# Mixing stage: the short convolution's chunks ahead of the attention's, the long convolution by channel halves, score groups every second slot from the 17th

## The chip, the cores and the metric

The kernel runs on one core of one Trainium2 chip. The metric is the device time of one execution in microseconds (us); lower is better.

## What is computed

A residual stream of 256 tokens by 1024 features goes through two layers of a first block and two layers of a second block. The change is in the first block's mixing stage, run once in each of its two layers. All data are float32.

```python
u = rms_norm(h, mix_pre_g[l])
(a_b, a_c, a_x, b_u, c_q, c_k, c_v, d_q, d_k, d_v, d_f, gate_logits) = _split(u @ w_in[l], IN_SPLITS)
y_a = (a_b * causal_depthwise_conv(a_c * a_x, a_conv_w)) @ a_w_out             # 3 taps, 512 channels
y_b = conformer_conv_mixer(b_u, ...)   # a * sigmoid(g), 31 taps on 512 channels, layer norm, silu, @ b_w_out
y_c = diff_attention_mixer(...)        # 4 heads, two softmaxes each, their difference @ v, rms norm, @ c_w_out
y_d = forgetting_attention_mixer(...)  # 8 heads, bias from a cumulative sum of log_sigmoid(d_f), @ d_w_out
g = sigmoid(gate_logits).reshape(bsz, seq, 4, D_MODEL)
merged = g[:, :, 0] * y_a + g[:, :, 1] * y_b + g[:, :, 2] * y_c + g[:, :, 3] * y_d
h = h + rms_norm(merged @ w_o[l], mix_post_g[l])
```

## The kernel before

**Chunks.** All weights stream through SBUF in 270 chunks of up to 128 x 2048 numbers, in the order `LOAD`, into a ring of `SLOTS = 5` buffers. SP issues the load of a chunk as soon as TensorE has used the chunk five earlier (L515). Each product is made of three fp32r products: ScalarE copies a chunk into `whi` (`split`, L575), VectorE subtracts it from the raw chunk into `wlo` in the raw chunk's place (`split`, L905), and `mm3` (L1433 to L1435) issues the three matmuls for each tile. The splits run `AHEAD = 3` chunks before their use.

**The mixing stage** has 47 slots, one chunk each: 23 `cols` chunks (`w_in` without the gates, in the order of the tuple `COLS`, whose numbers name the chunk: 14, 15, 0 and 1 to 3 are u and the long convolution's inputs with 0, 1 its gate halves; 4, 5, 6, 7 the short convolution's `a_c` and `a_x`; 8, 9 its `a_b`; 10 to 15 q, k, v of the first attention; 16 to 21 those of the second; 22 the forget logits; chunks 14 and 15 are taken by a routine of their own before slot 2), then 24 merge chunks: for each branch in the order a, c, d, b and each half of the features two `gate` chunks and one `out` chunk.

**Order of the work.** `mix_steps()` writes the steps between the chunks by hand: `at(slot, step)` puts a step ahead of that slot's chunk, and `rank` orders the steps of one slot. Every engine walks through the one list `MIX` and issues its own part of each step, in order; semaphores carry the rest. So within a slot

- TensorE does its transposes and small matmuls of the steps, then the slot's chunk (48 matmuls);
- ScalarE does its part of the steps, then empties the chunk's bank (an evacuation; L694 to L718, or a tanh, L728), then splits the chunk three slots on (L575);
- VectorE does its part of the steps, then what it has of the chunk (a masked product for `cols` 2, 3, 6, 7; the gated sum of an `out`, L1075 to L1080), then its split of the chunk three slots on (L905), which needs ScalarE's.

**The attention** goes in eight groups. Groups 0 to 3 are the first attention (0, 1 the first 128 queries with one tile of keys; 2, 3 the second 128 with two), 4 to 7 the second attention (4, 5 with two tiles of keys; 6, 7 with one). A group has four steps, in this kernel one slot after the other:

- `scores`: TensorE's score matmuls (L1675), VectorE's bias, maximum and its negation (L1178 or L1185, L1188, L1190), ScalarE's four exponentials (L768);
- `weigh`: VectorE's reciprocals and, in groups 0 to 3, the difference of the two softmaxes (L1198, L1201, L1205; L1210 in the others);
- `turn`: TensorE transposes the weights (L1690), ScalarE copies them (L775). TensorE waits for `p_ready` of this group's `weigh` and for `o_read` of the group before, which its `values` gives;
- `values`: TensorE's products with v (L1704), VectorE's normalization (L1218, L1223).

```python
                        pe.wait_ge(p_ready, l * 8 + (g + 1))
                        if g:
                            pe.wait_ge(o_read, l * 8 + g)
```

The first attention's output is then normalized (`o_norm` on ScalarE, L781, and POOL; `o_scale` on VectorE, L1232 and L1234), and all outputs are transposed (`flip`, L1716) and split (`o_split`, L789 and L1242). `conv` is one tap of the long convolution, four instructions on VectorE (L1094, L1096) and a drain behind them, `a_conv` one of the short one (L1108, L1110, L1114). Before slot 22's successor, the first gate chunk, TensorE waits for the evacuation of slot 22, since both use bank 0:

```python
                        if j:
                            pe.wait_ge(th_ready, l * 16 + ((j - 1) * 2 + part + 1))
                        else:
                            cols_taken(pe, l, COLS[22 - part])
```

Of the kernel before, what the change touches and what calls it, by code (L numbers as in the profile page):

```python
# [30 lines left out]
KH = HID // P  # L31
# [6 lines left out]
A_CONV = 3  # L38
B_CONV = 31
# [51 lines left out]

COLS = (14, 15, 0, 1, 2, 3, 22, 10, 11, 12, 13, 4, 5, 6, 7, 8, 9, 16, 17, 18, 19, 20, 21)
BRANCH = (0, 2, 3, 1)
HCOLS = (0, 1, 2, 5, 6, 7, 3, 4, 8, 9, 10, 11, 12, 13)

# [21 lines left out]
def mix_steps():  # L119
    before = {}  # L120

    def at(slot, *step):
        before.setdefault(slot, []).append(step)

    for tap in range(B_CONV):
        at(6 + tap * 28 // B_CONV, "conv", tap)
    for tap in range(A_CONV):
        at(15 + tap, "a_conv", tap)
    at(18, "a_split")
    at(35, "ln_stats")  # L130
    at(36, "ln_apply")
    at(38, "ln_back")
    at(39, "ln_silu")
    at(40, "ln_split")
    at(8, "f_turn")
    at(9, "f_log")
    at(10, "f_tok")
    at(12, "f_sum")
    at(13, "f_store")
    at(19, "f_load")  # L140
    at(21, "f_mask", 1)
    for g, s in enumerate((12, 14, 16, 18, 22, 24, 27, 29)):
        at(s, "scores", g)
        at(s + 1, "weigh", g)
        at(s + 2, "turn", g)
        at(s + 3, "values", g)
    at(25, "f_mask", 0)
    for i, s in enumerate((18, 22)):
        at(s, "o_norm", i)
        at(s + 1, "o_scale", i)  # L150
    for i, s in enumerate((21, 25, 29, 34)):
        at(s, "flip", i)
        at(s, "o_split", i)
    chunks = [("cols", i) for i in COLS]
    for b in range(4):
        for half in range(2):
            chunks += [("gate", b, half, 0), ("gate", b, half, 1), ("out", b, half)]
    rank = {"ln_stats": 0, "ln_apply": 0, "ln_back": 0, "ln_silu": 0, "weigh": 0, "values": 1, "flip": 2, "o_split": 3,
            "f_turn": 4, "f_sum": 4, "f_mask": 4, "turn": 5, "scores": 6}
    steps = []  # L160
    for slot, chunk in enumerate(chunks):
        steps += sorted(before.pop(slot, []), key=lambda x: rank.get(x[0], 8))
        steps.append(chunk)
    assert not before, before
    return steps


MIX = mix_steps()


# [70 lines left out]
def program(nc, stream, x_in, pre_gain, post_gain, par1, par2, cst_in, out):  # L241
    ctx = ExitStack()
    with ctx:
# [8 lines left out]
        at = nc.sbuf_base  # L252
# [29 lines left out]
        def area(a, n):  # L282
            return mix[:, a:a + n]
# [8 lines left out]
        PB = T + B_CONV - 1  # L292
        PA = T + A_CONV - 1
        pad_b = area(3072, KH * PB).rearrange("p (m t) -> p m t", m=KH)
        otok = [area(a, 1024).rearrange("p (a n) -> p a n", a=2) for a in (1024, 9336)]
        decay = area(5240, 2048).rearrange("p (e k) -> p e k", e=8)
        acc_b = area(4216, 1024).rearrange("p (m t) -> p m t", m=KH)
        lnt = area(4216, 1024).rearrange("p (t n) -> p t n", t=NT)
# [94 lines left out]
        conv_done = sem("conv_done")  # L393
# [501 lines left out]
        def _(dve):  # L895
# [121 lines left out]
            for l in range(DEPTH):  # L1017
# [22 lines left out]
                for step in MIX:  # L1040
                    kind = step[0]
                    if kind == "cols":
                        i = step[1]
                        p = COLS.index(i)
# [18 lines left out]
                    elif kind == "gate":  # L1063
                        _, b, half, part = step
                        at = AT_MERGE + (b * 2 + half) * 3 + part + AHEAD
                        split(ch + at)
                    elif kind == "out":
                        _, b, half = step
# [17 lines left out]
                                op0=ALU.mult, op1=ALU.subtract).then_inc(m_ready, 1)  # L1086
                        split(c + AHEAD)
                    elif kind == "conv":
                        tap = step[1]
                        for m in range(KH):  # L1090
                            w = pr1("b_conv")[:, m * B_CONV + tap:m * B_CONV + tap + 1]
                            v = pad_b[:, m, tap:tap + T]
                            if tap == 0:
                                ins = TS(acc_b[:, m, :], v, w, pr1("b_bias")[:, m:m + 1], ALU.mult, ALU.add)  # L1094
                            else:
                                ins = STT(out=acc_b[:, m, :], in0=v, scalar=w, in1=acc_b[:, m, :], op0=ALU.mult,  # L1096
                                          op1=ALU.add)
# [4 lines left out]
                    elif kind == "a_conv":  # L1102
                        tap = step[1]
# [63 lines left out]
                    elif kind == "scores":  # L1167
                        g = step[1]
# [22 lines left out]
                    elif kind == "weigh":  # L1191
                        g = step[1]
                        w, t, _ = group1(g)
# [18 lines left out]
                    elif kind == "values":  # L1212
                        g = step[1]
# [24 lines left out]
                    elif kind == "o_split":  # L1238
                        i = step[1]
# [9 lines left out]
            for l in range(DEPTH):  # L1249
# [40 lines left out]
                for step in HYB:  # L1290
# [3 lines left out]
                    elif kind == "chunk":  # L1294
                        _, p, i, half = step
# [7 lines left out]
                    elif kind == "a_norm":  # L1303
# [5 lines left out]
                        for t in range(NT):  # L1309
                            hyb_taken(dve, l, 2)  # L1310
                            x = z[:, t, Z_AQ:Z_AV].rearrange("p (e d) -> p e d", e=8)
                            for e0, e1, o in ((0, 6, 0), (6, 8, 128)):
                                a, b = (v[:, 64 * e0:64 * e1].rearrange("p (e d) -> p e d", d=64) for v in (thb, tmp))
# [44 lines left out]
                    elif kind == "scores":  # L1358
                        g = step[1]
# [21 lines left out]
                    elif kind == "weigh":  # L1381
                        g = step[1]
# [13 lines left out]
                    elif kind == "values":  # L1396
                        g = step[1]
# [28 lines left out]
        def _(pe):  # L1426
# [152 lines left out]
            for l in range(DEPTH):  # L1579
# [4 lines left out]
                for step in MIX:  # L1584
                    kind = step[0]
                    if kind == "cols":
                        i = step[1]
                        p = COLS.index(i)
# [5 lines left out]
                        if i == 22:  # L1594
                            s = c % SLOTS
# [9 lines left out]
                    elif kind == "gate":  # L1605
                        _, b, half, part = step
# [8 lines left out]
                    elif kind == "out":  # L1615
                        _, b, half = step
# [12 lines left out]
                        s = c % SLOTS  # L1629
# [5 lines left out]
                                          k == KH - 1)  # L1635
                        ins.then_inc(used, 1)
                    elif kind == "ln_stats":
                        pe.wait_ge(conv_done, l + 1)
                        for t in range(NT):
                            for m in range(KH):  # L1640
                                ins = pe.transpose(bank(4 + t)[:, m * P:(m + 1) * P], acc_b[:, m, t * P:(t + 1) * P],
# [22 lines left out]
                    elif kind == "scores":  # L1664
                        g = step[1]
# [6 lines left out]
                        for e in range(4):  # L1672

                            m, p0 = hp * 2 + e // 2, 64 * (e % 2)
# [3 lines left out]
                    elif kind == "turn":  # L1678
                        g = step[1]
                        w, t, _ = group1(g)  # L1680
# [6 lines left out]
                        n = 0  # L1687
# [322 lines left out]
```

## Time and profile before

| | |
|---|---|
| time, median of 3 runs | 1797.87 us (1796.89 to 1797.89) |
| the profiled execution's own time | 1796.47 us |
| its span | 1794.7 us |
| TensorE busy | 1707.2 us, 95% |
| VectorE busy | 1088.7 us, 61% |
| ScalarE busy | 800.2 us, 45% |
| mixing stage, end of slot 1 to end of slot 46 | 303.5 us in the first layer, 305.0 us in the second |

The profile is one execution. Its times are from the first to the last instruction; the execution's own time is 1.8 us longer. PE is TensorE's matmuls, PEld its weight loads, DVE VectorE, ACT ScalarE, POOL GpSimd. PEclk is the share of full speed that TensorE's clock was granted. A row that ends in [4.80 <-DVE mix L1218] says that the engine sat idle for 4.80 us before it, and that the instruction named released it.

### The profile page before, as it was taken

The numbers are of one execution on the slowest core, as the hardware profiler recorded it, in microseconds if no ns is written. First come the engines' busy times: TensorE is split into PE (matmuls) and PEld (weight loads), VectorE is DVE, ScalarE is ACT, GpSimd is POOL, SyncE is SP. The second block draws the span as 40 slices with busy tenths as digits, with TensorE's granted clock in tenths as the row PEclk, the third lists the DMA queues.
The fourth block names the chain that finished last, engine by engine and source line by source line (L and its number), as shares of the span: only waits on it lengthen the run. The fifth ranks groups of instructions, "written<-read, shape, count | busy, mean of one in ns | idle before, by whom it ended". The sixth has DMA issues, their size and how long they took to land.

```text
span 1794.7 us, 28417 instructions
## 1 busy us (share of the span) xinstructions
PE 1707.2 (95%) x12340; PEld 1597.0 (89%) x12340; DVE 1088.7 (61%) x1271; ACT 800.2 (45%) x1053; POOL 34.0 (2%) x60
## 2 busy tenths in 40 slices
PE   6999999789999999999999988999999999889987
PEld 6999899789999999899989978999999988679866
DVE  5454667777666444654466777766744466556554
ACT  5333544444444433534344444444533445544552
POOL 0000000000000000000000000000000000000000
PEclk9999999999999999999999989999999999999989
DMA  7555554334445555555545433445555542215120
GB/s 277 186 187 186 184 214 144 139 130 152 180 173 212 187 186 181 204 188 182 186 174 211 165 124 134 144 181 180 201 188 188 183 170 101 95 42 196 63 94 24
DMA packets 43358, 293.14 MB, mean 163 GB/s; under 512 B 4817, under 2 KB 5217, under 8 KB 10465
## 3 DMA queue, kind: packets, MB, share of 16 engines
q1 hardware_dynamic: 39744, 278.94, 43.1%
q10 hardware_dynamic: 3488, 12.38, 2.0%
q8 instruction: 98, 1.61, 0.4%
q14 instruction: 28, 0.22, 0.0%
HBM read 290.23 MB, written 1.06 MB: 162 GB/s over the span
## 4 chain that ended last, share of the span: by engine, by line
PE 81%; DVE 8%; ACT 7%; DVEq 2%; issue 2%; DMA 1%; POOL 0%; ACTq 0%; SPq 0%; POOLq 0%
PE ps L1433 24%; PE ps L1434 23%; PE ps L1435 23%; ACT whi L575 3%; DVE wlo L905 3%; DVEq L1187 1%; PE ps L1524 1%; PE ps L1822 1%; PE ps L1525 1%; PE ps L1532 1%; ACT prob L768 1%; PE ps L1848 1%; PE ps L1479 1%; PE ps L1704 1%; ACT tmp L578 1%
## 5 line engine op out<-in xcount | busy, mean ns | idle before, releaser
L905 DVE TENSOR_TENSOR wlo<-raw,whi 128x2048 fp32r<-128x2048 f32 (+2 forms) x270 | 603.8, 2242 | 429.2 <-ACT whi L575 423.5
L1433 PE MATMUL ps<-xhi,whi 128*128 128x256 f32 x2512 | 722.6, 288 | 10.1 <-ACT mix L718 9.2
L1434 PE MATMUL ps<-xlo,whi 128*128 128x256 f32 x2512 | 715.6, 285 | 0.0
L1435 PE MATMUL ps<-xhi,wlo 128*128 128x256 f32 x2512 | 715.5, 285 | 0.0
L575 ACT ACTIVATE whi<-raw 128x2048 fp32r<-128x2048 f32 (+2 forms) x270 | 498.6, 1866 | 15.9 <-DMA raw<-stream 15.4
L1433 PEld LDWEIGHTS ps<-xhi,whi 128*128 128x128 f32 x2512 | 485.8, 193 | 17.0 <-issue 13.5
L1434 PEld LDWEIGHTS ps<-xlo,whi 128*128 128x128 f32 x2512 | 485.8, 193 | 2.5
L1435 PEld LDWEIGHTS ps<-xhi,wlo 128*128 128x128 f32 x2512 | 485.3, 193 | 0.5
L1433 PE MATMUL ps<-whi,yar 128*128 128x512 f32 (+1 forms) x492 | 197.9, 402 | 14.5 <-ACT mix L820 7.6
L1434 PE MATMUL ps<-wlo,yar 128*128 128x512 f32 (+1 forms) x492 | 194.0, 394 | 0.0
L1435 PE MATMUL ps<-whi,yar 128*128 128x512 f32 (+1 forms) x492 | 193.4, 393 | 0.0
L629 ACT ACTIVATE thb<-ps 128x512 f32<-128x512 f32 x44 | 26.3, 597 | 287.8 <-PE ps L1435 275.9
L1433 PEld LDWEIGHTS ps<-whi,yar 128*128 128x128 f32 x492 | 93.7, 190 | 39.1 <-DVE wlo L905 15.7
L1435 PEld LDWEIGHTS ps<-whi,yar 128*128 128x128 f32 x492 | 93.9, 191 | 20.0
L1434 PEld LDWEIGHTS ps<-wlo,yar 128*128 128x128 f32 x492 | 94.0, 191 | 17.8 <-issue 0.6
L1096 DVE SCALAR_TENSOR_TENSOR mix<-mix,par 128x256 f32<-128x256 f32 x240 | 100.2, 480 | 2.3
L1433 PE MATMUL ps<-whi,xhi 128*128 128x256 f32 (+2 forms) x256 | 74.6, 291 | 3.5 <-DVE wlo L905 3.5
L638 ACT ACTIVATE yar<-tmp 128x512 fp32r<-128x512 f32 x40 | 25.3, 633 | 108.3 <-DVE tmp L972 108.3
L1433 PE MATMUL ps<-yar,whi 128*128 128x256 f32 x256 | 72.9, 285 | 0.0
L1434 PE MATMUL ps<-wlo,xhi 128*128 128x256 f32 (+2 forms) x256 | 72.8, 284 | 0.0
L1435 PE MATMUL ps<-whi,xlo 128*128 128x256 f32 (+2 forms) x256 | 72.7, 284 | 0.0
L1435 PE MATMUL ps<-yar,wlo 128*128 128x256 f32 x256 | 72.4, 283 | 0.0
(198 smaller groups left out, 1727.5 us busy)
## 6 DMA issues: line engine op xcount, KB each, us to landing
raw<-stream SPq DMA_DIRECT2D x254, 1024.0 KB, 4.8
raw<-stream SPq DMA_DIRECT2D x10, 768.0 KB, 4.2
gpre<-pre_gain ACTq DMA_DIRECT2D x9, 512.0 KB, 4.4
gpost<-post_gain ACTq DMA_DIRECT2D x6, 512.0 KB, 5.3
mix<-cum ACTq DMA_DIRECT2D x2, 1024.0 KB, 4.7
raw<-stream SPq DMA_DIRECT2D x2, 640.0 KB, 4.3
h<-x_in SPq DMA_DIRECT2D x2, 512.0 KB, 5.9
out<-mix SPq DMA_DIRECT2D x4, 256.0 KB, 2.1
```

What stands on the lines that cost most here:

```text
L575: A(whi[:, s, 0:w], raw[:, s, 0:w], ACT.Copy).then_inc(hi_ready, 1)
L578: A(tmp[:, n * 512:(n + 1) * 512], src, ACT.Square, scale=1.0 / 32, accum_out=rq[:, t, col + n:col + n + 1]).then_inc(sq_done, 1)
L629: A(silu, bank(0), ACT.Silu).then_inc(silu_done, 1)
L638: A(hhi[hbuf(g)].rearrange("p m t -> p (m t)"), src, ACT.Copy).then_inc(hhi_done, 1)
L768: ins = A(prob[:, e, 0:nk], prob[:, e, 0:nk], ACT.Exp, bias=small[:, g % 2, e:e + 1], scale=0.125, accum_out=small[:, g % 2, 4 + e:5 + e])
L905: TT(wlo[:, s, 0:w], raw[:, s, 0:w], whi[:, s, 0:w].bitcast(F32), ALU.subtract).then_inc(lo_v, 1)
L1096: ins = STT(out=acc_b[:, m, :], in0=v, scalar=w, in1=acc_b[:, m, :], op0=ALU.mult, op1=ALU.add)
L1187: dve.drain()
L1433: pe.matmul(dst, lh, rh, start=first, stop=False)
L1434: pe.matmul(dst, lh, rl, start=False, stop=False)
L1435: return pe.matmul(dst, ll, rh, start=False, stop=last)
L1479: ins = pe.transpose(bank(turn_bank(X, t) + k // 4)[:, k % 4 * P:(k % 4 + 1) * P], xn[:, t, k * P:(k + 1) * P], ident)
```

## The change

It reorders the steps of the mixing stage and splits each tap of the long convolution in two. Nothing is computed otherwise.

```diff
-COLS = (14, 15, 0, 1, 2, 3, 22, 10, 11, 12, 13, 4, 5, 6, 7, 8, 9, 16, 17, 18, 19, 20, 21)
+COLS = (14, 15, 0, 2, 1, 3, 22, 4, 5, 6, 7, 8, 9, 10, 11, 12, 13, 16, 17, 18, 19, 20, 21)
...
     for tap in range(B_CONV):
-        at(6 + tap * 28 // B_CONV, "conv", tap)
-    for tap in range(A_CONV):
-        at(15 + tap, "a_conv", tap)
-    at(18, "a_split")
+        at(4 + tap * 30 // B_CONV, "conv", tap, 0)
+        at(6 + tap * 28 // B_CONV, "conv", tap, 1)
+    for tap, s in enumerate((12, 13, 14)):
+        at(s, "a_conv", tap)
+    at(15, "a_split")
...
-    for g, s in enumerate((12, 14, 16, 18, 22, 24, 27, 29)):
+    for g, s in enumerate((17, 19, 21, 23, 25, 27, 29, 31)):
         at(s, "scores", g)
         at(s + 1, "weigh", g)
         at(s + 2, "turn", g)
         at(s + 3, "values", g)
...
-    for i, s in enumerate((18, 22)):
+    for i, s in enumerate((26, 28)):
         at(s, "o_norm", i)
         at(s + 1, "o_scale", i)
-    for i, s in enumerate((21, 25, 29, 34)):
+    for i, s in enumerate((28, 30, 32, 36)):
         at(s, "flip", i)
         at(s, "o_split", i)
...
-        otok = [area(a, 1024).rearrange("p (a n) -> p a n", a=2) for a in (1024, 9336)]
+        otok = [area(a, 1024).rearrange("p (a n) -> p a n", a=2) for a in (2048, 9336)]
...
-                        tap = step[1]
-                        for m in range(KH):
+                        _, tap, part = step
+                        for m in range(2 * part, 2 * part + 2):
```

The waits for the convolution's end count to two per layer (`conv_done`). The other steps move by little: `f_turn` 8 to 9, `f_store` 13 to 14, `f_load` 19 to 23, the two `f_mask` 21 and 25 to 25 and 28, `ln_apply` 36 to 35, `ln_back` 38 to 37, `ln_silu` 39 to 40, `ln_split` 40 to 41. `otok` of the first attention lies at 2048, where `a_b` was, since the merge now writes the area from 1024 while it is still in use. Lines from 1096 on carry a number higher by one in the changed kernel.

The first place is VectorE around a score group with two tiles of keys in the first attention. Before, slots 15 and 16 and the start of slot 17 (L905 is a split, L1178 to L1190 a group's `scores`, L1198 to L1205 a `weigh`, L1218 a `values`, L1096 the long convolution, L1108 and L1110 the short one):

```order
L905 TENSOR_TENSOR wlo<-raw,whi 128x2048
L1198 RECIPROCAL small<-small 128x4
L1201 SCALAR_TENSOR_TENSOR small<-small,lamb 128x2
L1205 SCALAR_TENSOR_TENSOR prob<-prob,small 128x128 x2
L1218 TENSOR_TENSOR mix<-ps,small 128x256
L1096 SCALAR_TENSOR_TENSOR mix<-mix,par 128x256 x8
L1108 TENSOR_SCALAR mix<-mix,par 128x256 x4
L905 TENSOR_TENSOR wlo<-raw,whi 128x2048
L1178 SCALAR_TENSOR_TENSOR prob<-cst,ps 128x512 x2
L1188 TENSOR_REDUCE small<-prob 128x4
L1190 TENSOR_SCALAR small<-small 128x4
```

The same group in the changed kernel, in slots 20 and 21:

```order
L906 TENSOR_TENSOR wlo<-raw,whi 128x2048
L1199 RECIPROCAL small<-small 128x4
L1202 SCALAR_TENSOR_TENSOR small<-small,lamb 128x2
L1206 SCALAR_TENSOR_TENSOR prob<-prob,small 128x128 x2
L1219 TENSOR_TENSOR mix<-ps,small 128x256
L1097 SCALAR_TENSOR_TENSOR mix<-mix,par 128x256 x4
L906 TENSOR_TENSOR wlo<-raw,whi 128x2048
L1179 SCALAR_TENSOR_TENSOR prob<-cst,ps 128x512 x2
L1189 TENSOR_REDUCE small<-prob 128x4
L1191 TENSOR_SCALAR small<-small 128x4
```

Between the two splits stand a `weigh`, a `values` and one tap in place of a `weigh`, a `values`, two taps and a tap of the short convolution.

The second place is ScalarE at the turn from the `cols` chunks to the gates, slots 21 to 23. Before (L718 is the evacuation of a v chunk, L728 a gate's tanh, L781 `o_norm`):

```order
L718 ACTIVATE mix<-ps 128x2x256
L575 ACTIVATE whi<-raw 128x2048
L768 ACTIVATE prob,small<-prob,small 128x256 x4
L781 ACTIVATE tmp,rq<-mix 128x128 x4
L718 ACTIVATE mix<-ps 128x2x256
L575 ACTIVATE whi<-raw 128x2048
L728 ACTIVATE thb<-ps 128x512
```

And in the changed kernel:

```order
L719 ACTIVATE mix<-ps 128x2x256
L576 ACTIVATE whi<-raw 128x2048
L719 ACTIVATE mix<-ps 128x2x256
L576 ACTIVATE whi<-raw 128x2048
L776 ACTIVATE probT<-ps 128x512
L769 ACTIVATE prob,small<-prob,small 128x256 x4
```

Nothing stands any more between the split of slot 21 and the evacuation of slot 22; the exponentials come one slot later.

## Rows read from the trace of the kernel before

**Rows 1.** The page: span, and busy time of each engine
```profile
span 1794.7 us, 28417 instructions
...
PE 1707.2 (95%) x12340; PEld 1597.0 (89%) x12340; DVE 1088.7 (61%) x1271; ACT 800.2 (45%) x1053; POOL 34.0 (2%) x60
```

**Rows 2.** Slots 2 to 46, both layers: us, busy PE PEld DVE ACT POOL, PEclk, DMA
```profile
221.40:524.90 303.50, 287.05 (x2347) 280.57 (x2347) 219.07 (x285) 136.49 (x185) 3.54 (x6) 0.98 0.45 164
943.10:1248.10 305.00, 289.99 (x2347) 283.51 (x2347) 219.06 (x285) 136.63 (x185) 3.54 (x6) 0.97 0.46 163
```

**Rows 3.** Waits of PE, first layer: total, times, longest
```profile
PE ps L1690 <- DVE mix L1218: 10.6, 3, 4.9
PE ps L1433 <- ACT mix L718: 4.6, 1, 4.6
PE ps L1690 <- DVE prob L1205: 1.2, 1, 1.2
```

**Rows 4.** The same, second layer (the row of L718 there reads as above)
```profile
PE ps L1690 <- DVE mix L1218: 9.5, 3, 4.8
...
PE ps L1690 <- DVE prob L1205: 0.9, 1, 0.9
```

**Rows 5.** Timeline of DVE around the first long wait: start, us, instruction [idle before]
```profile
297.47 0.87 DVE L1096 SCALAR_TENSOR_TENSOR mix<-mix,par 128x256 f32<-128x256 f32 x2
...
309.77 2.29 DVE L905 TENSOR_TENSOR wlo<-raw,whi 128x2048 fp32r<-128x2048 f32 x1
311.98 1.28 DVE L1178 SCALAR_TENSOR_TENSOR prob<-cst,ps 128x512 f32<-128x512 f32 x2
...
314.71 1.67 DVE L1096 SCALAR_TENSOR_TENSOR mix<-mix,par 128x256 f32<-128x256 f32 x4
...
319.24 2.29 DVE L905 TENSOR_TENSOR wlo<-raw,whi 128x2048 fp32r<-128x2048 f32 x1 [1.10 <-ACT whi L575]
321.45 0.17 DVE L1198 RECIPROCAL small<-small 128x4 f32<-128x4 f32 x1
...
322.95 0.42 DVE L1218 TENSOR_TENSOR mix<-ps,small 128x256 f32<-128x256 f32 x1
```

**Rows 6.** Timeline of ACT: two chunks' pace in slots 10 and 11, then the same place
```profile
270.73 0.60 ACT L716 ACTIVATE mix<-ps 128x512 f32<-128x512 f32 x1 [3.37 <-PE ps L1435]
...
276.49 0.60 ACT L698 ACTIVATE mix<-ps 128x512 f32<-128x512 f32 x1 [3.36 <-PE ps L1435]
...
304.23 0.60 ACT L702 ACTIVATE mix<-ps 128x512 f32<-128x512 f32 x1 [3.18 <-PE ps L1435]
...
314.84 0.51 ACT L768 ACTIVATE prob<-prob,small 128x256 f32<-128x256 f32 x1 [7.94 <-DVE small L1190]
...
316.82 0.58 ACT L702 ACTIVATE mix<-ps 128x512 f32<-128x512 f32 x1
317.30 1.90 ACT L575 ACTIVATE whi<-raw 128x2048 fp32r<-128x2048 f32 x1
```

**Rows 7.** Timeline of PE: the first long wait; a wait in the second block
```profile
323.53 0.95 PE L1690 MATMUL ps<-cst,prob 128*128 128x128 f32 x4 [4.80 <-DVE mix L1218]
...
1493.83 0.38 PE L1433 MATMUL ps<-whi,xhi 128*128 128x256 f32 x1 [1.73 <-DVE wlo L905]
```

**Rows 8.** Busy time by stretch: short waits, then half clock behind longer ones
```profile
290.00:322.00 32.00, 26.83 (x220) 25.62 (x220) 28.14 (x53) 13.15 (x25) 0.00 (x0) 1.00 0.44 152
323.70:327.10 3.40, 3.40 (x15) 2.24 (x14) 3.25 (x9) 0.60 (x1) 0.00 (x0) 0.50 0.03 5
...
1043.90:1050.70 6.80, 5.82 (x25) 4.69 (x26) 6.47 (x12) 0.60 (x1) 0.00 (x0) 0.50 0.03 13
...
1494.50:1497.80 3.30, 3.30 (x18) 3.30 (x17) 0.94 (x1) 0.53 (x1) 0.00 (x0) 0.50 0.37 154
```

**Rows 9.** Timeline of ACT before the first gate chunk
```profile
366.72 0.51 ACT L768 ACTIVATE prob<-prob,small 128x256 f32<-128x256 f32 x1 [5.10 <-DVE small L1190]
...
370.04 0.60 ACT L718 ACTIVATE mix<-ps 128x512 f32<-128x512 f32 x1
```

More of the change, by code:

```diff
@@ L125, in mix_steps @@
     for tap in range(B_CONV):
-        at(6 + tap * 28 // B_CONV, "conv", tap)
-    for tap in range(A_CONV):
-        at(15 + tap, "a_conv", tap)
-    at(18, "a_split")
-    at(35, "ln_stats")
[L131 to L135, printed above, removed]
+        at(4 + tap * 30 // B_CONV, "conv", tap, 0)
[3 more added lines that the diff above has]
+    at(15, "a_split")
+    at(35, "ln_stats")
+    at(35, "ln_apply")
+    at(37, "ln_back")
+    at(40, "ln_silu")
+    at(41, "ln_split")
+    at(9, "f_turn")
     at(9, "f_log")
@@ L138, in mix_steps @@
     at(12, "f_sum")
-    at(13, "f_store")
-    at(19, "f_load")
-    at(21, "f_mask", 1)
-    for g, s in enumerate((12, 14, 16, 18, 22, 24, 27, 29)):
+    at(14, "f_store")
+    at(23, "f_load")
+    at(25, "f_mask", 1)
+    for g, s in enumerate((17, 19, 21, 23, 25, 27, 29, 31)):
         at(s, "scores", g)
@@ L146, in mix_steps @@
         at(s + 3, "values", g)
-    at(25, "f_mask", 0)
-    for i, s in enumerate((18, 22)):
+    at(28, "f_mask", 0)
+    for i, s in enumerate((26, 28)):
         at(s, "o_norm", i)
         at(s + 1, "o_scale", i)
-    for i, s in enumerate((21, 25, 29, 34)):
+    for i, s in enumerate((28, 30, 32, 36)):
         at(s, "flip", i)
@@ L1637, in _ @@
                     elif kind == "ln_stats":
-                        pe.wait_ge(conv_done, l + 1)
+                        pe.wait_ge(conv_done, l * 2 + 2)
                         for t in range(NT):
```

## The prediction

> **What bounds the kernel now.** I read the page first: TensorE is busy for 1707.2 of 1794.7 us, VectorE for 61% and ScalarE for 45% [rows 1]. So time can only come from TensorE's idle stretches and from its slow ones. The list of its waits over the two mixing stages shows the few that are there: in the first layer 10.6 + 4.6 + 1.2 us and 0.4 us elsewhere, 16.8 us [rows 3]; in the second 9.5 + 4.6 us and 1.3 us of single short ones, 15.4 us [rows 4]. The reader is to see who releases TensorE: VectorE's `weigh` and `values` (L1205, L1218) ahead of a `turn`, and one evacuation (L718). The stretches by clock show the rest. Behind waits of 4.80 us the granted clock is 0.50 of full speed, the 1.2 GHz level, for 3.4 us in the first layer and for 6.8 us in the second; behind one of 1.73 us in the second block it falls too; through the stretch from 290 to 322 us, which holds the wait of 1.2 us and the shortest of the three on L1218 (10.6 less 4.8 and 4.9, so 0.9), it stays at 1.00 [rows 3, 7, 8]. Each mixing stage has three such falls of the length shown, one for each wait over 3 us.
>
> A floor follows. The first layer's slots 2 to 46 took 303.5 us [rows 2]. Less 16.8 us of waits and three falls at half of 3.4 us (5.1 us) that is 281.6 us, say 282, which no reordering of the same matmuls changes. A chunk takes 5.76 us of it (evacuations at 270.73 and 276.49, each released by its chunk's end) [rows 6].
>
> **Why the waits are there.** The timelines of ScalarE and VectorE around the first long one give the loop [rows 5, 6]. Slot 15's chunk ended at 304.2 (its evacuation starts at 304.23). VectorE began the split of that slot only at 309.77 and group 2's `scores` at 311.98, 7.8 us after the chunk. Scores took 2.73 us (to 314.71), the exponentials 1.98 us (314.84 to 316.82), evacuation 0.48, ScalarE's split 1.90 (to 319.20), VectorE's split 2.21 (319.24 to 321.45), `weigh` 1.50, `values` 0.42, to 323.37; TensorE's `turn` came at 323.53, 4.80 us late [rows 7]. On time, a slot's two splits are done 4.8 us after its chunk (0.1 + 0.5 + 1.9 + 2.3), not 7.8. The 3.0 us are what slot 15 holds on VectorE beyond its share: a second tap (1.74 us) and the short convolution's first. The third long wait is another: in slot 22 the evacuation that the first gate needs stands behind four exponentials and `o_norm` (366.72 to 370.04) [rows 9].
>
> **The change, by parts.** From such durations, each from its own row of the two timelines, I wrote out a timetable of slots 2 to 46: every engine takes its steps in the listed order, a step starts when its engine is free and what it waits for is there, 0.1 us after the signal. For the order before it gives long waits of 4.9, 4.8 and 4.5 us against 4.80, 4.9 and 4.6 in the trace, short ones of 1.1 and 0.9 for 1.2 and 0.9, and 303.3 us for the stage with a fall of 1.7 us behind each long wait; the trace has 303.5. One thing it shows counts later: the loss of the first fall is not paid, since the next `turn` is late by VectorE's chain anyway and waits 1.7 us less.
>
> *The short convolution ahead.* Its three taps (four instructions each, like those of the long one's), the product and the split of 1.2 us each, some 7 us on VectorE, leave slots 15 to 18 for slots 12 to 15, which now hold no attention. Summed over the timetable, slots 12 to 16 held 35.4 us of VectorE's steps on 33.7 us of TensorE's, waits left out; now 28.9 on 29.8. No wait comes of it. SP's loads and POOL's queue carry the same work in the same order of need.
>
> *Channel halves.* The 120 + 4 instructions stay, 31 drains become 62. Four in a row take 1.67 us and the next starts after 1.74; two take 0.87 [rows 5]. With 0.07 for the drain a half is 0.95 us, a tap 1.90 for 1.74: 4.7 us more VectorE work per layer. Bounds: nothing (0.875 a half), and 1.0 a half. In the timetable these move the stage by -1.0 and +1.1 us per layer. The first half's four earlier slots take that work off nobody: VectorE is idle for half of slots 4 and 5.
> The Trainium skill (VectorE: DVE Perf Modes, The DRAIN you can't avoid) says that the next operation does not start until the pipe is empty in any case, so that a halving would be free; the trace disagrees a little, since four instructions of 0.48 us follow each other in 1.67 us. By the skill the stage would be 1.0 us shorter per layer.
>
> *Groups every second slot.* Take group 2, now in slot 21, from the end of slot 20's chunk as 0. Slot 20 holds `weigh`, `values` and one tap, so both splits are done at 4.8. Scores to 7.5, exponentials to 9.6, evacuation and ScalarE's split to 12.0, VectorE's split to 14.3, `weigh` 15.8, `values` 16.3. TensorE: a wait of 0.8 for `turn` 1, then `turn` 1 and scores 1.6 and the chunk 5.76, to 8.1; `values` 0.4 and the next chunk, to 14.3. So `turn` 2 waits 2.1 us, not 4.8. The same way the other waits come out as 0.7 (slot 17, the first scores right behind their k chunk's evacuation), 1.3, 0.8, 2.1, 1.4, 1.9 (slots 19 to 27), and two `flip`s behind `o_scale` 0.6 and 1.0: 9.8 us per layer for 17.9. From group 4 on `weigh` costs 0.3 in place of 1.5 us and TensorE's own part of a pair is longer, so its turns wait no more.
>
> *The gate's wait* of 4.6 us goes: slot 22 holds no exponentials, and the 0.7 us that the evacuation needs lie beside the wait for `turn` 2.
>
> *The end.* Taps end in slot 33 as before. The last `flip` is in slot 36 for its product in slot 37: in the timetable its split is ready 1.7 us early, the second `flip` 3.4 us early; normalization and its product have one slot less and keep over 5 us. If TensorE gains, SP's loads come due sooner, but they are issued by use, so with it.
>
> **Sum.** 282 us, 7.8 us of waits and 3.4 us for falls behind the waits of 2.1 and 1.9 us (over the 1.73 us that brought one; one of the falls shortens the next wait from 1.4 to 0.2, which is why 9.8 reads 7.8): 293.2 us for 303.5 in the first layer. In the second the falls were twice as long; between 293.2 and, with two falls of 6.8 us, 296.6, I take 294.9 for 305.0. Together 20.4 us less. The profiled execution took 1796.5 us, so 1776.1; the median of the runs is 1.4 us higher, so 1777.5, and I say **1777 us**.
> The Trainium skill (TensorE: Matmul & The Clock Gate, Terms) prices a throttled time at its length times the share of the clock lost, each fall in full; the trace agrees for the second and third fall, not for the first. By it the first layer would end at 295.1, the sum at about 1780.
>
> **Rivals.**
> *No falls.* If waits of about 2 us leave the clock alone, as those of 1.2 and 0.9 us do [rows 8], the stage takes 291.7 us twice, 25.1 us less: 1772.8. Against it stands the fall behind 1.73 us.
> *Falls behind every wait over 0.7 us*, or 6.8 us long in both layers: 296.6 us twice, 15.3 us less: 1782.6. With 1.0 us per half 297.6: 1784.6.
> *Given back at the end.* Each of four products or transposes (slots 28, 30, 31, 37) late by one slot of 5.8 us takes back 23 us in all: 1798, no change. It needs VectorE 1.7 to 3.4 us behind the timetable there.
> *Slower: VectorE's backlog moves to slots 25 to 34.* The second attention, both `o_scale`, four `o_split`, two masks, three sums and the taps put 67.0 us of VectorE's steps on 72.7 of TensorE's. Should VectorE fall 3 us behind from group 1 on, all turns would come as those of slots 18 and 20 did, 4.8 us late: 8 x 4.8 = 38 for 17.9, 42 us more in both layers with falls hidden: about 1838. It decides if a pair of slots holds over 14.0 us for VectorE; I count 12.9 in the worst pair without an extra (two splits 4.4, four halves 3.8, scores 2.7, `weigh` and `values` 2.0), and an extra of 1.3 or 1.6 comes only in pairs where `weigh` is 0.3.
>
> **How the numbers follow.** 0.2% is 3.6 us, about what a measurement of this kernel can tell from no change. The forecast case has 0.50, no falls 0.15, more falls 0.25; all are faster. Given back has 0.05, slower 0.05. Of the first three, 0.01 may fall short of 3.6 us. The range takes in the no-fall case with free halves (1770.8), and reaches past 1784.6 to 1786 for a later `flip`.
>
> **What would show it.** Right: TensorE's waits in either stage between 8 and 11 us with none over 2.5 us; the one behind L719 gone; the turns of slots 19 to 27 still released by VectorE; VectorE busy about 4 us more in the stage; clock falls two per layer. Wrong: waits over 4 us on a `turn` or `flip` in slots 25 to 34, an `out` waiting for `y_ready`, or a first-layer stage over 300 us.

## The result, and the profile after

| | before | changed |
|---|---|---|
| time, median (lowest to highest) of 4 runs each | 1797.38 us (1792.13 to 1797.89) | 1768.01 us (1765.65 to 1771.01) |
| the profiled execution's own time | 1796.47 us | 1770.08 us |
| its span | 1794.7 us | 1768.3 us |
| mixing stage, first and second layer | 303.5, 305.0 us | 293.1, 292.8 us |
| second block, both layers | 333.2 us | 329.0 us |

The ratio of the times is 0.9842, 95% interval 0.9819 to 0.9865: faster by 1.6%. The time lies 9 us under the forecast and 2.0 us under the low end of its range.

Every line that these rows name is higher by one in the changed kernel, the split and the evacuation (L576, L719 for L575, L718) as well as those from 1096 on. The page of the changed kernel, span and busy time, against [rows 1]:

```profile
span 1768.3 us, 28477 instructions
...
PE 1695.9 (96%) x12340; PEld 1585.0 (90%) x12340; DVE 1093.3 (62%) x1271; ACT 800.4 (45%) x1053; POOL 36.8 (2%) x60
```

Busy time by stretch in the changed kernel: slots 2 to 46 of either layer, against [rows 2], then the two layers of the second block. The columns are the stretch, its length, busy time of PE, PEld, DVE, ACT and POOL, PEclk, DMA share and GB/s.

```profile
221.80:514.90 293.10, 284.37 (x2347) 277.72 (x2347) 221.34 (x285) 136.88 (x185) 4.94 (x6) 0.99 0.48 169
933.10:1225.90 292.80, 282.87 (x2347) 276.59 (x2347) 221.35 (x285) 136.73 (x185) 4.94 (x6) 1.00 0.48 170
1439.30:1599.20 159.90, 144.43 (x939) 124.00 (x938) 97.34 (x165) 80.80 (x162) 6.68 (x9) 0.97 0.31 108
1599.20:1768.30 169.10, 147.56 (x928) 126.75 (x927) 94.22 (x163) 75.01 (x155) 6.69 (x9) 0.93 0.24 84
```

The second block in the kernel before, the same columns:

```profile
1461.50:1626.10 164.60, 147.57 (x938) 127.20 (x938) 97.33 (x165) 80.96 (x162) 6.67 (x9) 0.95 0.30 105
1626.10:1794.70 168.60, 146.35 (x928) 126.23 (x927) 94.20 (x163) 75.03 (x155) 6.69 (x9) 0.94 0.24 85
```

The 26.4 us of the profiled execution are therefore 10.4 and 12.2 us in the two stages, 4.2 us in the second block, whose code is the same, less 0.4 us ahead of the first stage. VectorE has 4.6 us more to do over the span and the time fell all the same.

What TensorE waits for in the changed kernel (engine, line, total us, times, longest), first layer, against [rows 3]:

```profile
PE ps L1691 <- DVE mix L1219: 5.0, 3, 2.3
PE ps L1717 <- DVE mix L1235: 1.8, 2, 1.4
PE ps L1691 <- DVE prob L1206: 1.1, 1, 1.1
PE ps L1676 <- ACT mix L717: 0.7, 1, 0.7
```

and second layer, against [rows 4]:

```profile
PE ps L1691 <- DVE mix L1219: 6.0, 4, 2.0
PE ps L1717 <- DVE mix L1235: 1.8, 2, 1.0
PE ps L1691 <- DVE prob L1206: 1.4, 1, 1.4
```

The row of the gate's wait (4.6 us, L718) has no successor. All that is left are short waits: on the same chain, `weigh` and `values` ahead of a `turn` and `o_scale` ahead of a `flip`, and 0.7 us of the first scores for an evacuation (L717). The walk through group 2 can be checked row by row. VectorE in slots 20 to 22 of the changed kernel (start, us, instruction, idle before):

```profile
337.12 2.29 DVE L906 TENSOR_TENSOR wlo<-raw,whi 128x2048 fp32r<-128x2048 f32 x1 [0.43 <-ACT whi L576]
339.33 1.28 DVE L1179 SCALAR_TENSOR_TENSOR prob<-cst,ps 128x512 f32<-128x512 f32 x2
...
342.06 1.83 DVE L1097 SCALAR_TENSOR_TENSOR mix<-mix,par 128x256 f32<-128x256 f32 x4
346.58 2.29 DVE L906 TENSOR_TENSOR wlo<-raw,whi 128x2048 fp32r<-128x2048 f32 x1 [2.70 <-ACT whi L576]
348.79 0.17 DVE L1199 RECIPROCAL small<-small 128x4 f32<-128x4 f32 x1
...
350.30 0.42 DVE L1219 TENSOR_TENSOR mix<-ps,small 128x256 f32<-128x256 f32 x1
350.82 1.83 DVE L1097 SCALAR_TENSOR_TENSOR mix<-mix,par 128x256 f32<-128x256 f32 x4
```

and ScalarE beside it:

```profile
344.17 0.57 ACT L719 ACTIVATE mix<-ps 128x512 f32<-128x512 f32 x1
344.65 1.90 ACT L576 ACTIVATE whi<-raw 128x2048 fp32r<-128x2048 f32 x1
```

The split of slot 20 ends at 339.33, by the prediction's clock 4.8, so its zero is 334.53. From there the scores' results (342.06) come at 7.5, the exponentials' end (344.17) at 9.6, ScalarE's split (346.55) at 12.0, VectorE's split (348.79) at 14.3, `weigh` (350.30) at 15.8: the walk to a tenth. And the `turn` itself, on TensorE, which was idle from 348.53 on, by this clock 14.0 for the walk's 14.3; so the wait is 2.3 us for 2.1:

```profile
350.87 0.63 PE L1691 MATMUL ps<-cst,prob 128*128 128x128 f32 x4 [2.34 <-DVE mix L1219]
```

What followed this wait in the first layer, and what followed the same wait, 2.00 us long, in the second (stretches, columns as above; PEclk is the third number from the end):

```profile
351.90:355.30 3.40, 3.40 (x18) 2.67 (x15) 3.33 (x4) 0.23 (x1) 0.00 (x0) 0.50 0.29 120
1061.50:1066.00 4.50, 3.83 (x30) 3.32 (x31) 4.17 (x7) 1.70 (x2) 0.00 (x0) 1.00 0.53 218
```

A fall to 0.50 for 3.4 us behind the one, none behind the other, and none anywhere else in either stage.

### The profile page after: what moved, and what is told of

The parts are those of the page before. It is cut to its first block, busy times and chain, and to the rows that moved or that the text cites. A ratio compares the mean times of both kernels' runs of the same rounds, so it can differ in the third digit from the quotient of the medians.

```text
span 1768.3 us, 28477 instructions
## 1 busy us (share of the span) xinstructions
PE 1695.9 (96%) x12340; PEld 1585.0 (90%) x12340; DVE 1093.3 (62%) x1271; ACT 800.4 (45%) x1053; POOL 36.8 (2%) x60
## 4 chain that ended last, share of the span: by engine, by line
PE 75%; DVE 11%; ACT 6%; DVEq 4%; issue 2%; DMA 1%; POOL 0%; ACTq 0%; SPq 0%; POOLq 0%
PE ps L1434 22%; PE ps L1436 22%; PE ps L1435 22%; DVE wlo L906 4%; ACT whi L576 3%; PE ps L1823 2%; DVEq L1188 1%; PE ps L1525 1%; DVE mix L1097 1%; DVEq L1102 1%; PE ps L1526 1%; ACT prob L769 1%; PE ps L1533 1%; PE ps L1480 1%; PE ps L1834 1%
## 5 line engine op out<-in xcount | busy, mean ns | idle before, releaser
L576 ACT ACTIVATE whi<-raw 128x2048 fp32r<-128x2048 f32 (+2 forms) x270 | 498.3, 1866 | 14.0 <-DMA raw<-stream 13.3
L1434 PE MATMUL ps<-whi,yar 128*128 128x512 f32 (+1 forms) x492 | 196.5, 399 | 14.5 <-ACT mix L821 7.6
L1097 DVE SCALAR_TENSOR_TENSOR mix<-mix,par 128x256 f32<-128x256 f32 x240 | 105.2, 480 | 6.4 <-issue 0.9
L1434 PE MATMUL ps<-yar,whi 128*128 128x256 f32 x256 | 73.3, 286 | 0.0
L1435 PE MATMUL ps<-yar,whi 128*128 128x256 f32 x256 | 72.4, 283 | 0.0
```

Of the source, the lines that this page charges most:

```text
L576: A(whi[:, s, 0:w], raw[:, s, 0:w], ACT.Copy).then_inc(hi_ready, 1)
L1434: pe.matmul(dst, lh, rh, start=first, stop=False)
L1435: pe.matmul(dst, lh, rl, start=False, stop=False)
```

## The experiments

The first four ran together, with a median of 1795.75 us for the kernel before beside them; the next four together (before: 1796.58 us), and the last two (before: 1795.68 us), each of the three sets on another chip. A median is of 4 executions, of 10 in e5 and 8 in e8; the stages are those of one of them. In what follows "waits" are all idle time of TensorE in a stage, and "lost" the length of the falls times the missing half of the clock; where a fall begins before its wait has ended, that stretch is counted in both.

**The changed kernel again (e1).** No edit.

> The changed kernel once more, for the scatter of its own time. Theory (clock): VectorE's and ScalarE's timetable fixes the waits, so both stages again last 291.5 to 293.5 us with 9 to 10 us of waits, and what differs from look to look is only how often and where the clock falls behind the same waits; times of single runs lie on two or more levels some 4 to 6 us apart, and span less time lost to the clock stays within 2 us of the first look. Rival: the scatter comes from the weight stream (DMA), so spans differ at the same mean clock.

Measured: 1772.5 us, ratio 0.9871 (0.9853 to 0.9889). Stages 293.15 and 294.5 us; second block 330.3 us. Two rows of its stretches, the second stage and a place in the second block, with the timeline's row of the wait ahead of that place:

```profile
932.60:1227.10 294.50, 285.91 (x2348) 279.25 (x2347) 221.35 (x285) 137.01 (x185) 4.94 (x6) 0.99 0.47 169
1473.70:1477.10 3.40, 3.40 (x19) 3.40 (x17) 0.67 (x1) 0.27 (x1) 0.00 (x0) 0.50 0.27 113
```

```profile
1472.76 0.39 PE L1434 MATMUL ps<-whi,xhi 128*128 128x256 f32 x1 [1.73 <-DVE wlo L906]
```

The same wait and the stretch behind it in the first execution:

```profile
1471.64 0.39 PE L1434 MATMUL ps<-whi,xhi 128*128 128x256 f32 x1 [1.73 <-DVE wlo L906]
```

```profile
1472.50:1475.90 3.40, 3.40 (x25) 3.11 (x24) 0.75 (x1) 0.35 (x1) 0.00 (x0) 1.00 0.31 125
```

This is the run that teaches most. The wait is 1.73 us in both, at the same instruction, in one kernel; one execution falls behind it and the other doesn't. In the second stage too this profile has two falls, one of them behind a wait of 1.43 us, where the first had none; its 294.5 us lie outside the 291.5 to 293.5 expected. What a wait costs in clock is thus not a property of the wait.

**The long convolution's taps left out (e2).** Taps 13 to 29 of 31 are not computed. (In this run's rows, lines behind the edit are higher by two more.)

```diff
                         _, tap, part = step
+                        if 12 < tap < B_CONV - 1:
+                            continue
```

> The changed kernel without taps 13 to 29 of the long convolution (both halves; that part is left out, 68 instructions and their drains per layer). Theory (chain): the waits come from the chain evacuation, ScalarE's split, VectorE's split, weigh, values, and not from VectorE's load, so most of them stay: 6 to 7 us of waits per stage for 9 to 10, the one ahead of the third turn still 2.0 to 2.5 us; stage 3 to 4 us shorter, about 1763. Rival (load): VectorE is too full in slots 17 to 34; without 32 us of taps per layer no wait over 0.7 us stays, stage 283 to 284 us, about 1752.

Measured: 1761.51 us, ratio 0.9813 (0.9796 to 0.9831). Its first-layer stage and its waits:

```profile
220.90:510.50 289.60, 283.92 (x2347) 277.53 (x2347) 192.23 (x217) 136.89 (x185) 4.94 (x6) 0.99 0.48 171
```

```profile
PE ps L1693 <- DVE mix L1221: 4.2, 4, 2.1
PE ps L1693 <- DVE prob L1208: 0.8, 1, 0.8
PE ps L1678 <- ACT mix L717: 0.7, 1, 0.7
```

29 us less for VectorE per stage bring 3.6 us in the first stage, 6.5 us in the second (288.0 for 294.5 in e1, where e1 has two falls and this run none) and 11.0 us in all. The waits are 5.7 us in each stage for 8.7 and 8.6 in e1, a little under the 6 to 7 expected, and two of them are over 0.7 us by far (2.15 and 1.44), where the rival had none. The 2.15 us wait of `turn` 2 stays, since in its slots the tap fills time in which VectorE has to wait for ScalarE's split anyway (the 2.70 us in the timeline above). So about a third of the waits goes with the load; the longest one and most of the rest stand on the order in the chain.

**The short convolution late again (e3).**

```diff
-    for tap, s in enumerate((12, 13, 14)):
+    for tap, s in enumerate((15, 16, 17)):
         at(s, "a_conv", tap)
-    at(15, "a_split")
+    at(18, "a_split")
```

> The changed kernel with the short convolution's steps at slots 15, 16, 17 and its split at 18, as before the change. Theory: the last tap now stands between the first scores and the split of slot 17, so the first two turns come later (waits of 2.4 and 2.0 us for 1.3 and 0.8), 2.3 us more per stage, about 4.5 us in all if the clock does as before. Rival (the place of the short convolution does not matter once the groups start in slot 17): stages within 0.5 us of the changed kernel's.

Measured: 1776.55 us, ratio 0.9897 (0.9877 to 0.9916), 4.05 us over e1; stages 297.4 and 297.1 us. Its waits in the first layer:

```profile
PE ps L1691 <- DVE mix L1219: 6.1, 4, 2.0
PE ps L1691 <- DVE prob L1206: 2.1, 1, 2.1
PE ps L1717 <- DVE mix L1235: 1.2, 1, 1.2
```

`turn` 0 and `turn` 1 wait 2.08 and 2.04 us in place of 1.08 and 0.72; two falls more in the first layer do the rest. The two stages are 4.3 and 2.6 us longer than in e1, 6.9 us together, and the execution only 4.05 us, since the second block took 327.4 us for 330.3 here. So the place of these steps is worth 4 to 7 us in the new order; the chunks of the short convolution stay ahead in this run, and what moving them is worth by itself is not shown.

**`weigh` a slot earlier (e4).** In the changed kernel `weigh` is the first of the next slot's steps, behind the split. Here it is the last of its own slot's.

```diff
-        at(s + 1, "weigh", g)
+        at(s, "weigh", g)
...
-    rank = {"ln_stats": 0, "ln_apply": 0, "ln_back": 0, "ln_silu": 0, "weigh": 0, "values": 1, "flip": 2, "o_split": 3,
+    rank = {"ln_stats": 0, "ln_apply": 0, "ln_back": 0, "ln_silu": 0, "weigh": 9, "values": 1, "flip": 2, "o_split": 3,
```

> The changed kernel with each group's weigh in the slot of its scores, as VectorE's last step ahead of the split there (VectorE idles there for 2.2 us in the timetable, waiting for ScalarE). Theory (chain): 1.5 us leave the chain of the two splits; waits fall from 9.8 to about 4.9 us per stage, stage 286.9 us, some 10 us less in all: 1757 to 1761. Rival (load): VectorE has no idle time there, so its split comes later by as much and nothing is won (within 2 us of the changed kernel).

Measured: 1757.99 us, ratio 0.9797 (0.9782 to 0.9812). First-layer stage and waits:

```profile
220.90:508.40 287.50, 282.50 (x2347) 276.59 (x2347) 221.38 (x285) 136.67 (x185) 4.95 (x6) 1.00 0.48 173
```

```profile
PE ps L1691 <- DVE mix L1219: 2.8, 3, 1.7
PE ps L1717 <- DVE mix L1235: 1.6, 2, 1.1
```

With the same work on every engine, moving one step across VectorE's split takes 5.7 us off the first stage and 7.0 us off the second against e1, and no fall is left in either. That it is for the most part the chain that TensorE waits for, and not load, is shown by this run and e2 together: moving `weigh` takes 14.5 us off e1's time, leaving out 29 us of VectorE's work per stage 11.0.

**The kernel before again (e5).** No edit. It gives the scatter of stages and second block in the old order.

> The kernel before, once more. Theory (clock): the waits are fixed (16 to 17 us in each stage), the falls of the clock are not; the stages last 303 to 305.5 us, and the second block, whose code the change leaves alone, differs from the first look's 333.2 us by up to 5 us with the time lost at half clock, as it does between the looks at the changed kernel (329.0 and 330.3 us). Rival: the second block is always near 333 us in the kernel before, and the change shortens it by some means of its own.

Measured: 1797.27 us, ratio 1.0007 (0.9997 to 1.0017); stages 305.6 and 305.35 us, second block 333.2 us. The first stage, which took 303.5 us in the profile of before, has falls twice as long here (lost 10.2 for 5.1 us): here too the clock moves a stage by 2 us. It isn't more, since each of these falls begins 0.9 to 1.4 us before its wait has ended, and since the waits are 1.1 us shorter. The second block took 333.2 us again, as the rival has it.

**`weigh` and `o_scale` early (e6).** e4, with `o_scale` ahead of the slot's taps, both masks behind them, and the first of the two masks a slot earlier.

```diff
-    at(25, "f_mask", 1)
+    at(24, "f_mask", 1)
...
-            "f_turn": 4, "f_sum": 4, "f_mask": 4, "turn": 5, "scores": 6}
+            "o_scale": 7, "f_turn": 4, "f_sum": 4, "f_mask": 8.5, "turn": 5, "scores": 6}
```

> The kernel with weigh in the slot of its scores, and with o_scale and the first mask moved too: o_scale ahead of that slot's taps, the masks behind them and the first one slot earlier. Theory (chain): both waits of a flip for o_scale (0.7 to 1.1 us) go, the waits of the turns in slots 23 and 27 (0.9 and 1.6) stay; stage 286.0 us for 287.5, about 1755. Rival: VectorE's order matters no more, within 1 us of 1758.

Measured: 1756.35 us, ratio 0.9774 (0.9757 to 0.9791). First-layer stage and all its waits over 0.2 us:

```profile
221.50:507.00 285.50, 282.11 (x2347) 276.48 (x2347) 221.37 (x285) 136.60 (x185) 4.94 (x6) 1.00 0.49 174
```

```profile
PE ps L1691 <- DVE mix L1219: 2.7, 3, 1.6
PE ps L1676 <- ACT mix L717: 0.7, 1, 0.7
```

Both `flip` waits are gone, and the stages, 285.5 us each, are 2.0 us shorter than in e4 and 3.5 us over the floor of 282. The medians alone (1.6 us apart, on two chips, with intervals that overlap) would not show it. This is the fastest kernel of the study: 2.3% under the kernel before, and some 12 to 16 us under the changed one.

**Whole taps (e7).** The changed kernel with the long convolution as it was: each tap in one piece, 31 drains.

```diff
-        at(4 + tap * 30 // B_CONV, "conv", tap, 0)
-        at(6 + tap * 28 // B_CONV, "conv", tap, 1)
+        at(6 + tap * 28 // B_CONV, "conv", tap)
```

> The changed kernel with the long convolution's taps whole again (four instructions and one drain, slots 6 to 33). Theory: the halving costs VectorE 0.16 us per tap and wins nothing, but VectorE idles in most slots; the timetable has the waits at 10.0 for 9.8 us, stage within 1 us of the changed kernel's (292.0 for 291.7 without falls). Rival (halves are what wins, since a half gets in between and the first half starts earlier): stage 2 us longer or more. Rival (drains cost): stage 1 us shorter or more.

Measured: 1771.1 us, ratio 0.9858 (0.9839 to 0.9876), against 0.9871 for e1; stages 293.5 and 293.4 us. First layer:

```profile
220.70:514.20 293.50, 285.67 (x2348) 278.57 (x2348) 218.88 (x285) 136.99 (x185) 4.95 (x6) 0.99 0.47 169
```

VectorE is busy 2.5 us less per stage (218.88 for 221.34) and the time is the same. The channel halves give and cost nothing that can be measured.

**The groups a slot later (e8).** Every group, `o_norm`, mask and the first three `flip`s one slot later in the changed kernel, the last `flip` where it was.

```diff
-    for g, s in enumerate((17, 19, 21, 23, 25, 27, 29, 31)):
+    for g, s in enumerate((18, 20, 22, 24, 26, 28, 30, 32)):
```

> The changed kernel with the groups at slots 18, 20 to 32 and what hangs on them a slot later. Theory: exponentials stand ahead of slot 22's evacuation again, so the first gate waits (1.6 us), the product in slot 31 waits for the second flip's split (3.8 us), the last flip waits 1.7 us; waits 16 us per stage, stage 298 us without falls and up to 301 with them: 1780 to 1788. Rival (only the distance of the groups counts, not the slot they start in): within 2 us of the changed kernel.

Measured: 1787.74 us, ratio 0.9956 (0.9943 to 0.997); stages 302.2 and 302.35 us, second block 333.5 us. Waits in the first layer:

```profile
PE ps L1691 <- DVE mix L1219: 4.2, 3, 2.1
PE ps L1434 <- issue: 3.7, 1, 3.7
PE ps L1434 <- ACT mix L719: 1.8, 1, 1.8
PE ps L1717 <- DVE mix L1224: 1.7, 1, 1.7
```

This is the prediction's "given back at the end", made to happen: the first product of slot 31 comes late by 3.7 us (its row names no releaser), the gate's wait is back with 1.8 us, the last `flip` waits 1.7 us. What it waited for can be read from the code and two rows: an `out` of this branch waits for `y_ready`, which `o_split` on VectorE (L1243) gives, and that one ended at 420.98, 0.10 us before the product:

```profile
420.29 0.69 DVE L1243 TENSOR_TENSOR yar<-ps,yar 128x512 fp32r<-128x512 f32 x1
421.08 0.55 PE L1434 MATMUL ps<-yar,whi 128*128 128x256 f32 x1 [3.74 <-issue]
```

Starting at 17 and not at 18 is worth 9.0 and 7.9 us in the two stages, against e1. The profile of e8 is of its second longest execution, 1792.42 us, 4.7 us over its median.

**The kernel before with `weigh` early (e9).** The edit of e4 in the old order.

> The kernel before, with the weighing of a group's exponentials a slot earlier and ahead of the slot's convolution on VectorE (the edit that took the flips' waits out of the changed kernel). My theory (a stage is 282 us of TensorE plus the waits on late links of the groups' chain, plus the clock's falls behind long waits): the two waits on the flip and gate side that hang on the weighing shrink, the gate's 4.6 us stays since it hangs on the mask and the scaling; stages near 298.4 and 298.4 in place of 303.5 and 305.0, the execution 8 to 12 us under the kernel before, near 1787. Rival (the groups' pace alone made the waits, the weighing's place counts only in the changed order): within 2 us of the kernel before.

Measured: 1784.37 us, ratio 0.9941 (0.9919 to 0.9962), 11.3 us under the kernel before; stages 297.2 and 298.5 us. Waits in the first layer, all over 0.2 us:

```profile
PE ps L1690 <- DVE mix L1218: 7.3, 3, 3.8
PE ps L1433 <- ACT mix L718: 4.6, 1, 4.6
```

The chain explains the old order as well: the two long turns shrink from 4.8 and 4.9 to 3.8 and 3.3 us, and the gate's wait, which hangs on ScalarE's steps in slot 22, doesn't move.

**The changed kernel, third profile (e10).** No edit.

> The changed kernel once more, nothing edited, for the second block alone. If the second block is shorter by the change (rival), it is again below 331 us, as in the first two looks (329.0 and 330.3) against 333.2 in both looks at the kernel before. If it is only where the clock's falls lie (my theory), it may lie anywhere from 327 to 333.5, with the same 31 to 33 us of waits, and the execution's time follows span times the missing share of the clock. Both stages 292.8 to 295. Time 1766 to 1773.

Measured: 1768.61 us, ratio 0.9856 (0.9836 to 0.9876); stages 293.15 and 293.2 us, second block 328.0 us. The second block:

```profile
1438.80:1598.30 159.50, 142.96 (x939) 123.67 (x938) 97.32 (x165) 80.97 (x162) 6.67 (x9) 0.98 0.31 108
1598.30:1766.80 168.50, 146.29 (x929) 126.17 (x927) 94.18 (x163) 75.06 (x155) 6.69 (x9) 0.94 0.24 85
```

Three profiles of the changed kernel gave 329.0, 330.3 and 328.0 us for the second block, two at the kernel before and one at e9 333.2, 333.2 and 333.1. The 3 to 5 us did not come in one place: in the first and third profile in its first layer (4.7 and 5.1 us), in e1 in its second (2.6 us). Over the block the lost time was 17.0, 17.1 and 13.7 us for 18.7, the waits 30.8, 31.9 and 32.6 us for 33.0. So part of the gain is falls that landed elsewhere, the rest waits of the same code that came out shorter. In the first profile these are the waits right behind long falls: at the one wait of 3.79 us in each layer the clock fell for 10.2 us, where before it fell twice for 3.4 us, and the next wait (L1806, L1807 in the changed kernel) was 1.13 and 1.23 us long for 2.75 and 2.37.

Whether the new order brings the gain on average is open. The rivals of e5 and e10 say that it does, and both runs came out as they have it (333.2 us in the kernel before, 328.0 in the changed one); the theory of e10 allowed for either. Of the kernel before, 11 of the 33 executions beside the experiments took 1791.7 to 1793.1 us and the others 1795.4 to 1797.7; both of its profiles (1796.47 and 1798.11 us) are of the longer kind, so its second block was not seen in a shorter execution. For the rival speak all profiles of the new order but one: e2, e3, e4, e6 and e7 gave 327.4 to 330.3 us. Against it stands e8, which has the new order but for a slot and took 333.5. Sorted by when the block begins, those that began by 1447.6 us took 327.4 to 330.3 and those from 1449.0 us on 333.1 to 333.5. No run tests whether that is more than chance, and what decides where a fall lands was not found.

## Why the prediction was right, and where it failed

The mechanism was right: TensorE's late `turn`s and its wait at the first gate were shortened as worked out, and nothing was given back. The step that failed is the clock: its term in "Sum" took too much for the second stage, nothing for the second block, and the range left the scatter out. The single points:

- **What bounds the kernel.** Right. TensorE's waits and falls were the whole of what a reordering could win. Less waits and lost time, the changed stages are 282.7 and 282.9 us for the floor of 282.
- **The waits.** Predicted 9.8 us per layer (7.8 where a fall shortens the next wait); measured 8.7 and 9.9 us:

| slot | 17 | 19 | 21 | 23 | 25 | 27 | 28 | 30 |
|---|---|---|---|---|---|---|---|---|
| predicted, us | 0.7 | 1.3 | 0.8 | 2.1 | 1.4 | 1.9 | 0.6 | 1.0 |
| first layer | 0.69 | 1.08 | 0.72 | 2.34 | 0.12 | 1.94 | 0.47 | 1.36 |
| second layer | 0.69 | 1.44 | 0.72 | 2.00 | 1.34 | 1.94 | 0.81 | 1.00 |

- **A fall that isn't paid.** Right: behind the fall of slot 23 in the first layer the wait of slot 25 is 0.12 us, in the second, with no fall, it is 1.34. The layers took 293.1 and 292.8 us. By the Trainium skill (TensorE: Matmul & The Clock Gate, Terms), which charges a throttled time in full, they would lie 1.7 us apart; the trace shows 0.3.
- **The short convolution.** No wait of its own, as said; the place of its steps is worth 4 to 7 us (e3).
- **The channel halves.** Priced right: two halves take 1.83 us and the next split starts at 352.73, 1.91 us after their start, for 1.90. VectorE has 4.6 us more over both layers where the sum had 4.7 per layer and the list of signs "about 4 us more in the stage": of the 0.16 us that a tap takes longer, half shows as busy and half as idle time of 0.075 us at the drain, which is not counted. What it does to the time is nothing that e7 could measure; the bounds of -1.0 and +1.1 us a layer are no larger than the scatter of the stages. The prediction read the Trainium skill (VectorE: DVE Perf Modes, The DRAIN you can't avoid) as making the halving free. That section has an exception which the prediction left out, that a next operation that is not held starts earlier, and with it there is no disagreement with the trace: four instructions of 0.48 us take 1.67 us in a row, and 1.83 us with a drain between the halves.
- **The gate's wait.** Gone, as said.
- **The end.** No product or `flip` after slot 30 waits for more than 0.2 us. e8 shows how near it was: one slot later and 3.7 us of it come back in slot 31.
- **The sum, where it failed.** First stage 293.2 us predicted, 293.1 measured. To come so near was luck in part: the sum had 282 + 7.8 + 3.4, and the trace has 282.7 + 8.7 + 1.7, one fall and not two. The step that failed is the clock's term in "Sum". For the second stage it took 294.9 us, between one reading of the falls and a worse one; it took 292.8, 294.5 and 293.2 us in three profiles, with none, two and one fall, where the signs had two per layer. The worse reading was too dear in itself, since it priced falls of 6.8 us in full. In the trace before, 282 us, 15.0 of waits and three such falls in full make 307.2 us for a stage of 305.0 [rows 2, 8]. The first of these falls began at 1043.90, and its wait ended 0.98 us later:

```profile
1044.88 0.66 PE L1690 MATMUL ps<-cst,prob 128*128 128x128 f32 x2 [4.80 <-DVE mix L1218]
```

  In the other two it was 1.2 and 1.4 us, and these parts of the falls cost nothing, since TensorE was idle anyway. (The waits of 16.8 and 15.4 us in the prediction are 16.45 and 15.0 by [rows 2], length less PE's busy time; the floor of 282 us comes out the same.)

  Beyond the stages the sum had no term at all, while the second block took 2.9 to 5.2 us less than before. For the profiled execution that is -0.1 - 2.1 - 4.2 + 0.4 = -6.0 us, from 1776.1 to the measured 1770.1. The reading behind it was that a fall belongs to a wait over some length, learnt from one wait of 1.73 us [rows 7, 8]. e1 shows that very wait with a fall and the first profile without one.
- **The median and the range, where they failed too.** The profiled execution was 1.4 us under the median before and 2.1 us over it after: 3.5 us more. The 1.4 us were scatter themselves: beside the experiments the kernel before had medians of 1795.7 to 1796.6 us, against the profile's 1796.5. The four runs of the changed kernel show what that is: spans of 1768.3, 1764.0, 1763.8 and 1769.2 us at mean clocks of 0.989, 0.993, 0.992 and 0.988. Span times the missing share is 19.5 and 21.2 us in the two longer, 12.3 and 14.1 us in the two shorter, and what is left lies within 3.7 us (1748.0 to 1751.7; a clock rounded to 0.001 is good to 0.9 us either way). The range left this scatter out: it was built of the stages' cases alone, and 5 us more on either side would have been its due.
- **The rivals.** "No falls" was what the second layer did, with 292.8 for 291.7 us; with it in both layers the rival had 1772.8 us, still 4.8 over the result, so the stages alone can't account for the miss. "Given back" and "slower" didn't come (the 23 us of the first are one layer's; four times 5.8 us in both would be 46): no `turn` waits over 2.4 us, and in slots 25 to 34 no wait exceeds 1.94. The sum with the full price for each fall by the Trainium skill (TensorE: Matmul & The Clock Gate, Terms), about 1780, lies 12 us over the result, farther than the forecast.

## What to carry to other kernels

Follow one late instruction back through its engines' queues, slot by slot, with durations from the trace: such a walk gave eight waits to 0.4 us (the one behind a fall with the fall worked in), and moving the one step that stands on the wrong side of a long instruction (`weigh` behind the split) took off more (14.5 us) than leaving out 17 of the 31 taps on that engine (11.0 us). A step that only follows a 2.2 us split because the list says so should be tried ahead of it first. Price a fall of the clock as a chance, not as a mark of a wait's length, put the falls of the unchanged code into the range, and compare kernels by several executions: here the same program scatters by 5 us, for the most part through them.

## What the runs showed of the hardware that was not expected

The same wait of 1.73 us at the same instruction is followed by 3.4 us at half clock in one execution and by full clock in another (e1 and the first profile). In the second stage of the changed kernel the wait of 1.94 us ahead of slot 27's `turn` passed without a fall in the first profile and had one in the third (e10), and the wait of 1.43 us in slot 19 had one in e1 where 1.44 us had none in the first profile. And in code that was not touched the two layers of the second block took 159.5 to 164.7 and 165.6 to 169.1 us, by where the falls lay. Nor does a fall begin at a fixed time behind its wait: in the first stage of the kernel before one began 0.16 us behind the wait's end (323.69 for 323.53), in the second stage one 1.4 us ahead of it (1091.69 for 1093.13), in e1 one 1.24 us behind it (1033.41 for 1032.17).
